# Moving seven of the modulation's twelve column sums between the stages, with three accumulators and two weight buffers

## The chip, the cores and the metric

One core of one Trainium2 chip runs the whole program. The metric is the device time of one execution, in microseconds (us). The engines are TensorE (PE, with its weight loads PEld), VectorE (DVE), ScalarE (ACT), GpSimd (POOL) and SyncE (SP), whose queue issues nearly all DMAs.

## What is computed

Two blocks follow one another on a sequence of 256 tokens of width 1024, all in float32. The first block is a mixer (eight attention heads and four mLSTM heads) and a squared-ReLU MLP of width 4096, each with a norm ahead and one behind. The second block has two layers with a modulation:

```python
c_act = jax.nn.silu(c)
for l in range(DEPTH_2):
    mod = c_act @ ada_w[l] + ada_b[l]
    shift1, scale1, gate1, shift2, scale2, gate2 = [
        m[:, None, :] for m in jnp.split(mod, N_MOD, axis=-1)]
    h = rms_norm_2(x, norm1_g[l]) * (1.0 + scale1) + shift1
    z = h @ w_in[l]
    ...
    x = x + (1.0 + gate1) * mixed
    h2 = rms_norm_2(x, norm2_g[l]) * (1.0 + scale2) + shift2
    f_gate, f_up = jnp.split(h2 @ w_ffn_in[l], 2, axis=-1)
    x = x + (1.0 + gate2) * ((jax.nn.silu(f_gate) * f_up) @ w_ffn_out[l])
return rms_norm_2(x, final_g)
```

`c` is one row of 1024 numbers and `ada_w[l]` is 1024 x 6144, so `mod` is a vector of 6144 numbers for each layer. It depends on nothing but inputs, and its weights are 2 x 24 MB.

## The kernel before, in words

**Weights in chunks.** All large products go over one list of 168 chunks (`plan`). A chunk is 512 columns of a weight by up to four tiles of 128 rows, 1 MB, and lands in one of three slots of `raw` (`RING = 3`). Each chunk is split for a product in three parts: ACT rounds it to `hi` (L830), DVE subtracts to get `lo` (L1203), and PE runs 48 matmuls (L425): `hi` by the activations' high part, `lo` by the high part, `hi` by the low part. PE's program is the list of chunks in order, so it is the order of everything else. Chunks 0 to 11 are the first mixer's inputs, 12 to 15 its output ("out", half), 16 to 31 ("up", g), 32 to 47 ("down", half); then layer 0: 48 to 65 its inputs, 66 to 69 two branches, 70 to 73 its output, 74 to 95 its FFN, 96 to 107 its down product (the last chunk of each half has two tiles); layer 1 is 108 to 167 in the same way.

**Who waits for what.** ACT and DVE run two chunks ahead (`LEAD = 2`): DVE's `advance(c)` makes `lo` of chunk c+2. ACT's `split(c)` needs the raw chunk landed and its slot of `hi` free, that is, chunk c-3 finished by PE. SP issues the load of chunk c once DVE has finished `lo` of chunk c-3.

**The modulation.** Its weights come in 96 pieces of 128 rows by 1024 columns (`ADA_W`), 512 KB each; eight pieces make one of twelve groups, and group 6 l + q is one sixth of layer l's `mod`. DVE multiplies a piece by `c_act` (one scalar for each partition) and adds it into an accumulator: L1222 for a group's first piece, L1224 for the others. There are two accumulators, taken in turn, and three buffers for pieces (`ADA_RING = 3`). After the eighth piece PE sums the accumulator over its partitions, 128 columns at a time: eight matmuls with one column of ones (L489), into PSUM bank 2. DVE adds the bias (`ada_columns`, L1212).

**Where they stand.** `ada_pos[j]` is the chunk at whose `advance` DVE works on piece j; `ada_at[c]` is the group that PE sums right after chunk c. Five groups are spread over chunks 14 to 45 (one piece a chunk up to 31, then three for two chunks), six over layer 0's FFN and down (three for two chunks), and one over layer 1's FFN. On SP's queue the piece stands three chunks ahead of its use, and the load of a chunk stands behind it:

```python
while j < pieces and ada_pos[j] + 3 == c:
    if j >= ADA_RING:
        sp.wait_ge(sem("ada_used"), j - ADA_RING + 1)
    sp.dma_start(ada_raw[:, j % ADA_RING, :], src)
    j += 1
...
sp.dma_start(raw[:, c % RING, 0:nk, at:at + w], src)
```

**Between stages.** At each norm PE sums squares (`sum_squares`, `sum_squares_late`, L503, L519 and L527), then ACT forms the root, DVE scales and ACT makes the high part, and only then can PE start the next product. In that time PE runs `keep_warm`: four matmuls of 256 columns whose result nobody reads (L534), eight ahead of ("up", 0).

## Time and profile before

| | us |
|---|---|
| median of three runs | 1131.62 |
| lowest and highest of them | 1130.69, 1134.76 |
| the profiled execution | 1129.57 |
| its span in the trace | 1127.7 |
| busy in the span: PE, DVE, ACT | 1095.7, 814.1, 520.3 |
| moved by DMA | 229.67 MB, mean 204 GB/s |

The 1.9 us between the profiled execution's time and its span are start and end of the program. A busy engine is not one that sets the time: what counts is whose work the others wait for at each place, which the chain of waits tells. PE's granted clock was 1.00 of full speed in all stretches shown below.

### The profile page before, as it was taken

The page shows a single profiled execution, that of the slowest core. Times are in us where ns is not written, and L with a number is a line of the kernel's source. Part 1 is how long each engine was busy: PE and PEld are TensorE (multiplying, and loading weights), DVE is VectorE, ACT ScalarE, POOL GpSimd, SP SyncE. Part 2 cuts the span into 40 slices and gives each one's busy share as a digit, 9 for nine tenths or more (in the row PEclk, how much of TensorE's full clock was granted, in tenths as well). Part 3 has the DMA queues.
Part 4 walks back from the last instruction along what each step waited for, and adds up shares of the span by engine and source line. Part 5 has one row for each costly group of instructions (what it writes and reads, how often), then busy time and mean ns, then how long its engine had stood idle before and what let it go on. Part 6 is the DMA issues. An engine that isn't in the chain of part 4 may idle for free.

```text
span 1127.7 us, 19577 instructions
## 1 busy us (share of the span) xinstructions
PE 1095.7 (97%) x8420; PEld 1038.0 (92%) x8420; DVE 814.1 (72%) x1078; ACT 520.3 (46%) x609; POOL 12.0 (1%) x26
## 2 busy tenths in 40 slices
PE   6999999999999999999999999999999999999998
PEld 5877889999998988989999999999898899999998
DVE  4865579887765898966778787859989477656452
ACT  4545566453433544554544443354345355444441
POOL 4000000000000000000000000000000000000000
PEclk9999999999999999999999999999999999999999
DMA  7545346887984453406698989946442376676551
GB/s 217 164 136 180 120 168 235 289 279 267 329 306 144 150 169 131 150 32 234 204 315 281 360 304 336 309 129 222 152 150 76 112 242 219 204 250 206 169 169 38
DMA packets 132078, 229.67 MB, mean 204 GB/s; under 512 B 5993, under 2 KB 59607, under 8 KB 131993
## 3 DMA queue, kind: packets, MB, share of 16 engines
q1 hardware_dynamic: 130404, 227.11, 59.7%
q8 instruction: 66, 1.08, 0.4%
q10 hardware_dynamic: 917, 1.27, 0.4%
q0 software_dynamic: 672, 0.06, 0.1%
q14 instruction: 19, 0.16, 0.0%
HBM read 227.35 MB, written 1.06 MB: 203 GB/s over the span
## 4 chain that ended last, share of the span: by engine, by line
PE 72%; DVE 19%; ACT 5%; issue 2%; DMA 2%; SPq 0%; DVEq 0%; ACTq 0%
PE mm L425 63%; DVE lo L1203 6%; DVE cacc L1283 5%; ACT hi L830 3%; PE pv L489 2%; PE mm L464 2%; DMA raw<-in_w_out_dram 1%; DVE ada_acc L1224 1%; DVE sB L1291 1%; PE pa L527 1%; PE pv L745 1%; PE pa L519 1%; DVE pB L1652 1%; DMA xin<-in_x_dram 1%; DVE qk L1307 0%
## 5 line engine op out<-in xcount | busy, mean ns | idle before, releaser
L425 PE MATMUL mm<-act_hi,hi 128*128 128x256 f32 x1760 | 490.9, 283 | 6.3 <-ACT act_hi L898 2.7
L425 PE MATMUL mm<-act_hi,lo 128*128 128x256 f32 x1760 | 484.7, 279 | 0.0
L1203 DVE TENSOR_TENSOR lo<-raw,hi 128x2048 fp32r<-128x2048 f32 (+1 forms) x160 | 361.8, 2265 | 161.9 <-ACT hi L830 159.9
L425 PE MATMUL mm<-act_lo,hi 128*128 128x256 f32 x1760 | 467.4, 279 | 0.0
L830 ACT ACTIVATE hi<-raw 128x2048 fp32r<-128x2048 f32 (+1 forms) x160 | 301.5, 1890 | 240.2 <-PE mm L425 188.5
L425 PEld LDWEIGHTS mm<-act_hi,hi 128*128 128x128 f32 x1760 | 330.9, 188 | 12.5 <-issue 8.8
L425 PEld LDWEIGHTS mm<-act_hi,lo 128*128 128x128 f32 x1760 | 330.9, 188 | 0.9 <-issue 0.7
L425 PEld LDWEIGHTS mm<-act_lo,hi 128*128 128x128 f32 x1760 | 320.5, 188 | 0.0
L425 PE MATMUL mm<-u_hi,hi 128*128 128x256 f32 x608 | 170.7, 281 | 0.0
L425 PE MATMUL mm<-u_hi,lo 128*128 128x256 f32 x608 | 169.7, 279 | 0.0
L425 PE MATMUL mm<-u_lo,hi 128*128 128x256 f32 x608 | 169.7, 279 | 0.0
L425 PEld LDWEIGHTS mm<-u_hi,lo 128*128 128x128 f32 x608 | 114.3, 188 | 0.1
L425 PEld LDWEIGHTS mm<-u_hi,hi 128*128 128x128 f32 x608 | 114.3, 188 | 0.1
L425 PEld LDWEIGHTS mm<-u_lo,hi 128*128 128x128 f32 x608 | 114.3, 188 | 0.0
L1224 DVE SCALAR_TENSOR_TENSOR ada_acc<-ada_raw,ca,ada_acc 128x1024 f32<-128x1024 f32 x84 | 107.6, 1281 | 1.3 <-DMA ada_raw<-in_ada_w_dram 0.3
L1283 DVE SCALAR_TENSOR_TENSOR cacc<-cu,convw,cacc 128x256 f32<-128x256 f32 x240 | 98.9, 479 | 2.4
L1151 ACT ACTIVATE sq<-mm 128x512 f32<-128x512 f32 x22 | 13.2, 599 | 60.5 <-PE mm L425 60.5
L909 ACT ACTIVATE pB<-sB,small 128x128 f32<-128x128 f32 (+1 forms) x32 | 14.3, 449 | 50.4 <-DVEq L1295 50.4
L1251 DVE TENSOR_TENSOR u_lo<-sq,u_hi 128x512 fp32r<-128x512 f32 (+1 forms) x30 | 25.0, 835 | 16.9 <-ACT u_hi L902 16.6
L902 ACT ACTIVATE u_hi<-sq 128x512 fp32r<-128x512 f32 x22 | 13.9, 633 | 43.9 <-DVEq L1713 43.9
L1601 DVE SCALAR_TENSOR_TENSOR x<-mm,cols,x 128x256 f32<-128x256 f32 x32 | 14.0, 480 | 27.5 <-PE mm L425 26.9
L425 PE MATMUL mm<-on,raw 128*128 128x256 f32 x128 | 29.1, 380 | 0.2
(254 smaller groups left out, 962.3 us busy)
## 6 DMA issues: line engine op xcount, KB each, us to landing
ada_raw<-in_ada_w_dram SPq DMA_DIRECT2D x96, 512.0 KB, 6.2
raw<-in_w_ffn_in_dram SPq DMA_DIRECT2D x88, 512.0 KB, 5.8
raw<-in_w_in_dram SPq DMA_DIRECT2D x40, 1024.0 KB, 5.1
raw<-in_w_ffn_out_dram SPq DMA_DIRECT2D x20, 1024.0 KB, 5.9
raw<-in_w_up_dram SPq DMA_DIRECT2D x16, 1024.0 KB, 6.7
raw<-in_w_down_dram SPq DMA_DIRECT2D x16, 1024.0 KB, 7.8
raw<-in_w_out_dram SPq DMA_DIRECT2D x12, 1024.0 KB, 5.1
raw<-in_w_in_dram SPq DMA_DIRECT2D x16, 512.0 KB, 6.1
```

The lines of the kernel that those rows point to most:

```text
L425: ins = pe.matmul(o, w[:, kk, fs], a[:, k, :], start=(k == 0 and i == 0 and f % 2 == 0), stop=(ends and i == len(pairs) - 1), skip_group_c ...
L464: ins = pe.matmul(mm[:, b0 + tt, :], a[:, k, tok], w[:, kk, :], start=(k == 0 and i == 0), stop=(ends and i == 2), skip_group_check=True)
L489: ins = pe.matmul(b[:, f:f + 1], ada_acc[:, i % 2, f * P:(f + 1) * P], ones[:, 0:1], start=(f == 0), stop=True, skip_group_check=True)
L830: a(act.activation(hi[:, c % RING, 0:nk, :], raw[:, c % RING, 0:nk, :], ACT.Copy), "hi_done")
L902: a(act.activation(dst, src, ACT.Copy, scale=scale), done)
L909: a(act.activation(p[:, i, lo_:hi_], s[:, i, lo_:hi_], ACT.Exp, scale=-1.0, bias=small[:, 2 + 2 * i + q:3 + 2 * i + q], accum_out=small[:, ...
L1151: a(act.activation(sq[:, 0:2, :], complete((l, "ffn", g))[:, 0, :], other(ACT.Silu)), "silu_gate_ready")
L1203: v(dve.tensor_tensor(lo[:, c % RING, 0:nk, :], raw[:, c % RING, 0:nk, :], hi[:, c % RING, 0:nk, :].bitcast(F32), ALU.subtract), "lo_done")
L1224: link(dve.scalar_tensor_tensor(out=acc, in0=w, scalar=ca[:, 1, k:k + 1], in1=acc, op0=ALU.mult, op1=ALU.add), "ada_used")
L1251: ins = dve.tensor_tensor(d_lo, src, h, ALU.subtract)
L1283: v(dve.scalar_tensor_tensor(out=cacc[:, k, :], in0=src, scalar=w, in1=cacc[:, k, :], op0=ALU.mult, op1=ALU.add), name)
L1601: ins = dve.scalar_tensor_tensor(out=x[:, k, :], in0=tile_of(src, f), scalar=gain[:, k:k + 1], in1=x[:, k, :], op0=ALU.mult, op1=ALU.add)
```

## The change

Seven groups (0, 3, 4, 5, 9, 10 and 11) are no longer summed after a chunk but between stages: group 0 ahead of ("up", 0), groups 3 and 4 ahead of layer 0's input, 5 ahead of layer 0's FFN, 9 and 10 ahead of layer 1's input, 11 ahead of layer 1's FFN. The groups 1, 2, 6, 7 and 8 stay after chunks 22, 30, 79, 85 and 90. `keep_warm` is shorter at four of these places and gone at one. The eight pieces of group 0 stand at chunks 4 to 11, inside the first mixer, and all others move up by eight, so layer 1's FFN has none. There is a third accumulator (4 KB a partition), and `ada_raw` has two buffers in place of three.

```diff
--- before.py
+++ after.py
@@ -53,7 +53,8 @@
 ADA_W = D
 ADA_T = ADA_W // P
 ADA_GROUPS = MODS // ADA_T
-ADA_RING = 3
+ADA_RING = 2
+ADA_ACCS = 3
 ADA_P = KD
 LAMBDA_INIT = [0.8 - 0.6 * float(np.exp(-0.3 * l)) for l in range(LAYERS)]
 MAGIC = 1.5 * 2.0 ** 23
@@ -177,17 +178,20 @@
 
     first = {name: ids[0] for name, (_, ids) in groups.items()}
     pieces = LAYERS * ADA_GROUPS * ADA_P
-    stages = [(range(groups[("out", 0)][1][1], first[(0, "in", 3)]), 5, lambda c: 0.85 if c < first[("down", 0)] else 1.3)]
-    for l, after_ffn in ((0, 6), (1, 1)):
-        stages.append((range(first[(l, "ffn", 0)], first[(1, "in", 3)] if l == 0 else first[(1, "down", 0)]), after_ffn,
-                       lambda c: 1.0 if c < first[(0, "down", 0)] else 0.9))
+    stages = [(range(first[("in", 2)], first[("out", 1)] + 1), 1, lambda c: 1.0),
+              (range(groups[("out", 0)][1][1], first[(0, "in", 3)]), 5, lambda c: 0.85 if c < first[("down", 0)] else 1.3),
+              (range(first[(0, "ffn", 0)], first[(1, "in", 3)]), 6, lambda c: 1.0 if c < first[(0, "down", 0)] else 0.9)]
+    ada_between = {first[("up", 0)]: (0, 0, 1), first[(0, "in", 3)]: (0, 3, 2), first[(0, "ffn", 0)]: (0, 5, 1),
+                   first[(1, "in", 3)]: (1, 3, 2), first[(1, "ffn", 0)]: (1, 5, 1)}
+    later = {(l, q + i) for l, q, count in ada_between.values() for i in range(count)}
     ada_pos, ada_at = [], {}
     for window, count, share in stages:
         until = np.cumsum([share(c) for c in window[:-2]])
         for j in range(count * ADA_P):
             ada_pos.append(window[int(np.searchsorted(until, (j + 0.5) / (count * ADA_P) * until[-1]))])
-            if j % ADA_P == ADA_P - 1:
-                ada_at[ada_pos[-1] + 1] = divmod(len(ada_pos) // ADA_P - 1, ADA_GROUPS)
+            l, q = divmod(len(ada_pos) // ADA_P - 1, ADA_GROUPS)
+            if j % ADA_P == ADA_P - 1 and (l, q) not in later:
+                ada_at[ada_pos[-1] + 1] = l, q, 1
 
 
 
@@ -242,7 +246,7 @@
         hi = sb("hi", [P, RING, CK, GF], F32R)
         lo = sb("lo", [P, RING, CK, GF], F32R)
         ada_raw = sb("ada_raw", [P, ADA_RING, ADA_W])
-        ada_acc = sb("ada_acc", [P, 2, ADA_W])
+        ada_acc = sb("ada_acc", [P, ADA_ACCS, ADA_W])
         cst = sb("cst", [P, C_ALL])
         x = sb("x", [P, KD, S])
         act_hi = sb("act_hi", [P, KD, S], F32R)
@@ -480,15 +484,21 @@
                             ins.then_inc(sem(done), 1)
                 ins.then_inc(sem("mm_done"), 1)
                 if c in ada_at:
-                    l, q = ada_at[c]
-                    i = l * ADA_GROUPS + q
-
+                    ada_sums(c, ada_at)
+
+            def ada_sums(c, where, part=None):
+
+                l, q, count = where[c]
+                for a in range(count) if part is None else (part,):
+                    i = l * ADA_GROUPS + q + a
                     pe.wait_ge(sem("ada_used"), (i + 1) * ADA_P)
-                    b = bank(2)
+                    b = bank(2) if a == 0 else pv[2]
                     for f in range(ADA_T):
-                        ins = pe.matmul(b[:, f:f + 1], ada_acc[:, i % 2, f * P:(f + 1) * P], ones[:, 0:1], start=(f == 0), stop=True,
+                        to = a * ADA_T + f
+                        ins = pe.matmul(b[:, to:to + 1], ada_acc[:, i % ADA_ACCS, f * P:(f + 1) * P], ones[:, 0:1], start=(to == 0), stop=True,
                                         skip_group_check=True)
-                    full(ins, 2)
+                    if a == count - 1:
+                        full(ins, 2)
 
             def product(name, *acts, **kw):
                 for j in range(len(groups[name][1])):
@@ -691,7 +701,8 @@
             out_pieces(0, (4, 5, 6, 7))
             chunk(("out", 1), 1, act_hi, act_lo)
             sum_squares_late(((6, 7),))
-            keep_warm(WARM + 4)
+            ada_sums(first[("up", 0)], ada_between)
+            keep_warm(WARM + 0)
             for g in range(8):
                 product(("up", g), act_hi, act_lo, ready="norm_ready" if g == 0 else None)
                 if g == 0:
@@ -706,9 +717,12 @@
             for late in (True, False):
                 if late:
                     sum_squares_late(((6, 7),))
+                    ada_sums(first[(0, "in", 3)], ada_between, 0)
+                    keep_warm()
                 else:
                     sum_squares()
-                keep_warm()
+                    ada_sums(first[(0, "in", 3)], ada_between, 1)
+                    keep_warm(2)
 
 
             for l in range(LAYERS):
@@ -777,14 +791,15 @@
                     for half in range(2):
                         chunk((l, "out", half), j, act_hi, act_lo, ready=None if half else "mixed_split", per=2)
                 sum_squares_late()
-                keep_warm()
+                ada_sums(first[(l, "ffn", 0)], ada_between)
+                keep_warm(2)
                 for g in range(11):
                     product((l, "ffn", g), act_hi, act_lo, ready="norm_ready" if g == 0 else None)
                 product((l, "down", 0), u_hi, u_lo, ready="u_ready", per=2)
                 if l < LAYERS - 1:
                     product((l, "down", 1), u_hi, u_lo)
                     sum_squares_late()
-                    keep_warm()
+                    ada_sums(first[(1, "in", 3)], ada_between)
 
             def turn_output(kh, to):
 
@@ -1205,16 +1220,16 @@
 
             def ada_columns(c):
 
-                if c not in ada_at:
-                    return
-                l, q = ada_at[c]
-                mc = slice(l * MODS + q * ADA_T, l * MODS + (q + 1) * ADA_T)
-                link(dve.tensor_tensor(modT[:, mc], full(2)[:, 0:ADA_T], adabT[:, mc], ALU.add), "bank2_free")
+                for where in (ada_at, ada_between):
+                    if c in where:
+                        l, q, count = where[c]
+                        mc = slice(l * MODS + q * ADA_T, l * MODS + (q + count) * ADA_T)
+                        link(dve.tensor_tensor(modT[:, mc], full(2)[:, 0:count * ADA_T], adabT[:, mc], ALU.add), "bank2_free")
 
             def ada_piece(j):
 
                 i = j // ADA_P
-                acc = ada_acc[:, i % 2, :]
+                acc = ada_acc[:, i % ADA_ACCS, :]
                 dve.wait_ge(sem(f"ada_loaded{j % ADA_RING}"), 16 * (j // ADA_RING + 1))
                 k = j % ADA_P
                 w = ada_raw[:, j % ADA_RING, :]
```

Two places show what moved. The first is PE's program at the norm ahead of layer 1's input product, behind the last chunk of layer 0's down product. Before:

```order
L425 MATMUL mm<-u_hi,hi 128x256
L425 MATMUL mm<-u_hi,lo 128x256
L425 MATMUL mm<-u_lo,hi 128x256
L527 MATMUL pa<-sq,cst 128x256 x4
L534 MATMUL pv<-cst 128x256 x4
L425 MATMUL mm<-act_hi,hi 128x256
L425 MATMUL mm<-act_hi,lo 128x256
```

With the change (L537 and L498 are the lines that were L527 and L489):

```order
L429 MATMUL mm<-u_hi,hi 128x256
L429 MATMUL mm<-u_hi,lo 128x256
L429 MATMUL mm<-u_lo,hi 128x256
L537 MATMUL pa<-sq,cst 128x256 x4
L498 MATMUL pv<-cst,ada_acc 128x1 x16
L429 MATMUL mm<-act_hi,hi 128x256
L429 MATMUL mm<-act_hi,lo 128x256
```

The sixteen matmuls of groups 9 and 10 stand in the place of the four of `keep_warm`; their former places, each eight matmuls after a chunk of layer 0's down product, hold nothing now.

The second is DVE's program in the first mixer, at the step of chunk 4 (`advance(4)`). `nlam<-pv` frees PSUM bank 2 for PE's next product. Before:

```order
L1307 TENSOR_TENSOR qk<-qk,hf 128x512
L1203 TENSOR_TENSOR lo<-raw,hi 128x2048
L1376 COPY nlam<-pv 128x2
L1291 ISA sA,small<-pv,cst 128x128
L1291 ISA small 128x1
L1291 ISA sA,small<-pv,cst 128x256
```

With the change:

```order
L1322 TENSOR_TENSOR qk<-qk,hf 128x512
L1218 TENSOR_TENSOR lo<-raw,hi 128x2048
L1237 TENSOR_SCALAR ada_acc<-ada_raw,ca 128x1024
L1391 COPY nlam<-pv 128x2
L1306 ISA sA,small<-pv,cst 128x128
L1306 ISA small 128x1
L1306 ISA sA,small<-pv,cst 128x256
```

The first piece of group 0 (L1237, which was L1222) now stands ahead of that copy; seven more follow, one at each of the next seven chunks. SP's program has the same kinds of entries in the stages that follow; what differs there is the number that each piece waits for.

## Rows read from the trace of the kernel before

**Rows 1.** the chain of waits that ended last, by engine

```profile
PE 72%; DVE 19%; ACT 5%; issue 2%; DMA 2%; SPq 0%; DVEq 0%; ACTq 0%
```

**Rows 2.** by stretch: PE, PEld, DVE, ACT, POOL busy, clock, DMA share, GB/s

```profile
255.00:350.00 95.00, 95.00 (x819) 95.00 (x818) 67.56 (x46) 35.13 (x24) 0.00 (x0) 1.00 0.85 295
600.00:660.00 60.00, 60.00 (x518) 60.00 (x517) 48.60 (x39) 24.64 (x21) 0.00 (x0) 1.00 0.95 318
940.00:1040.00 100.00, 100.00 (x860) 100.00 (x859) 63.20 (x46) 45.80 (x37) 0.00 (x0) 1.00 0.70 227
```

**Rows 3.** the chain of waits in order of time: start, us, what

```profile
161.25 3.45 PE pv L534 x16
...
581.87 1.29 DVE ada_acc L1224
583.21 1.95 PE pv L489 x16
585.15 33.72 PE mm L425 x288
618.87 1.68 PE pv L489 x16
```

**Rows 4.** timeline, PE at the norms ahead of two products

```profile
546.07 1.89 PE L534 MATMUL pv<-cst 128*128 128x256 f32 x8
...
548.48 0.35 PE L425 MATMUL mm<-act_hi,hi 128*128 128x256 f32 x1 [0.52 <-ACT act_hi L898]
...
748.29 1.89 PE L534 MATMUL pv<-cst 128*128 128x256 f32 x8
...
751.11 0.36 PE L425 MATMUL mm<-act_hi,hi 128*128 128x256 f32 x1 [0.93 <-ACT act_hi L898]
```

**Rows 5.** timeline, first mixer: DVE's nlam and PE's gate product

```profile
59.78 0.15 DVE L1376 COPY nlam<-pv 128x2 f32<-128x2 f32 x1
...
60.08 3.62 PE L621 MATMUL pv<-hng,wg 128*36 128x256 f32 x16 [1.29 <-DVE nlam L1376]
```

**Rows 6.** waits of the SP queue: waited for, us in total, times, longest

```profile
SPq L373 <- DVE ada_acc L1224: 184.3, 74, 6.5
```

**Rows 7.** timeline, layer 0's FFN: the two pieces that bound a loop

```profile
615.27 1.28 DVE L1224 SCALAR_TENSOR_TENSOR ada_acc<-ada_raw,ca,ada_acc 128x1024 f32<-128x1024 f32 x1
...
628.44 1.28 DVE L1224 SCALAR_TENSOR_TENSOR ada_acc<-ada_raw,ca,ada_acc 128x1024 f32<-128x1024 f32 x1
```

**Rows 8.** timeline, layer 0's down: one loop (DVE, SP, ACT, DVE)

```profile
667.26 2.60 DVE L1224 SCALAR_TENSOR_TENSOR ada_acc<-ada_raw,ca,ada_acc 128x1024 f32<-128x1024 f32 x2
...
668.93 0.43 SPq L383 DMA_DIRECT2D raw<-in_w_ffn_out_dram  x1
...
675.57 1.92 ACT L830 ACTIVATE hi<-raw 128x2048 fp32r<-128x2048 f32 x1 [2.46 <-DMA raw<-in_w_ffn_out_dram]
...
679.80 1.28 DVE L1224 SCALAR_TENSOR_TENSOR ada_acc<-ada_raw,ca,ada_acc 128x1024 f32<-128x1024 f32 x1
```

**Rows 9.** timeline, first block's down: one loop (DVE, SP, DVE)

```profile
285.60 0.75 DVE L1222 TENSOR_SCALAR ada_acc<-ada_raw,ca 128x1024 f32<-128x1024 f32 x1
...
286.74 0.44 SPq L383 DMA_DIRECT2D raw<-in_w_down_dram  x1
...
299.45 1.28 DVE L1224 SCALAR_TENSOR_TENSOR ada_acc<-ada_raw,ca,ada_acc 128x1024 f32<-128x1024 f32 x1
```

**Rows 10.** landing of raw in 440 to 470, of ada_raw at 250.9

```profile
DMA to landing us min/median/max: 4.9/5.0/5.0
...
DMA to landing us min/median/max: 3.7/3.7/3.7
```

**Rows 11.** timeline, DVE's low parts in layer 0's FFN: first, third and fifth

```profile
578.34 2.29 DVE L1203 TENSOR_TENSOR lo<-raw,hi 128x2048 fp32r<-128x2048 f32 x1 [1.18 <-ACT hi L830]
...
589.49 2.29 DVE L1203 TENSOR_TENSOR lo<-raw,hi 128x2048 fp32r<-128x2048 f32 x1 [1.18 <-ACT hi L830]
...
601.38 2.29 DVE L1203 TENSOR_TENSOR lo<-raw,hi 128x2048 fp32r<-128x2048 f32 x1 [1.18 <-ACT hi L830]
```


## Prediction

> **What bounds the kernel now.** I read the chain of waits by engine first: TensorE (PE) holds 72% of it and VectorE (DVE) 19% [rows 1]. The table of stretches then says where PE stands without a gap: in the first block's down products, in the FFN of layer 0 and in that of layer 1 PE is busy for the whole stretch at a granted clock of 1.00, while the DMA share is 0.85, 0.95 and 0.70 [rows 2]. So in these stages only work taken off PE, or a wait put in front of it, moves the time; and in two of them the DMA engines are nearly full. The chain in order of time gives PE's rhythm: 288 matmuls in 33.72 us, which is six chunks of 48, so 5.62 us a chunk and **11.24 us for two**, and between them a column sum of 1.68 us that nothing hides [rows 3].
>
> **The change part by part.**
>
> *Seven column sums leave the chunk stream.* Each of the twelve sums is eight matmuls of L489 (16 records), 1.68 us on the chain [rows 3]. Three leave the first block's down products, three layer 0's FFN and down, one layer 1's FFN: 7 x 1.68 = **-11.8 us**.
>
> *They come back at five places between stages.* There PE waits for the norm and runs filler (L534: eight of them, 16 records, take 3.45 us, so 0.43 each [rows 3]). From the first filler matmul to the first matmul of the FFN it is 2.41 us in layer 0, and 2.82 us ahead of layer 1's input product [rows 4]. Ahead of both FFNs and at the second place ahead of layer 0's input, PE now has 1.68 + 2 x 0.43 = 2.54 us to do: 0.13 us too much, three times (I take the places not shown as like the one shown). Ahead of ("up", 0), eight fillers become one sum and four fillers, 3.40 for 3.45 us: nothing. The other place ahead of layer 0's input has one sum and its old four fillers, in a wait for x: nothing. Ahead of layer 1's input there are two sums, 3.36 us in 2.82: 0.54. Together **+0.9 us**. If a norm were ever shorter than its filler, each sum would cost its 1.68.
>
> *Eight pieces move into the first mixer.* A piece is one DVE instruction of 1.28 us (0.75 for the first of eight). Layer 1's FFN loses eight; PE did not wait for them there. The first new one stands on DVE between the low part of a chunk and the copy of nlam, which ends when PE starts L621 [rows 5]: **+0.8 us**. The other seven come once a chunk, where PE has a whole chunk of matmuls in front of it and DVE idles; I cost them at nothing (bounds: 0 and 7 x 1.28 = 9.0 us). Their DMAs go ahead of the weight chunks on SP's queue, whose chunks there are long landed when ACT takes them.
>
> *Two weight buffers for three.* This is the edit that decides. SP issues piece j ahead of the chunk three places on, and the next chunk's load is queued behind it. With three buffers, j waits until DVE has used piece j-3, with two until j-2. Even now SP waits 184 us in all for pieces [rows 6]. In the stretches with three pieces to two chunks, piece j-3 nearly always belongs to the chunk five ahead of the one loaded, whose low part the load waits for anyway; j-2 belongs to the chunk four ahead. That closes a loop over **two** chunks: piece used, ada and raw transfer, ACT's high part, DVE's low part, next piece used. It must fit into 11.24 us.
>
> The trace of before holds three such loops, at places where two chunks with two pieces each follow one another:
> - FFN: piece ended at 615.27 + 1.28 = 616.55, next piece ended at 628.44 + 1.28 = 629.72: **13.17 us** [rows 7].
> - down of layer 0: first of two pieces ended at 668.54, raw issued at 668.93, next piece ended at 681.08: **12.54 us** [rows 8].
> - down of the first block: 286.35 to 300.73, **14.38 us** [rows 9]; older loads were still under way, so it is the upper bound.
>
> The lower bound is from idle stretches: a piece alone lands 3.7 us after its issue, a raw chunk alone in 5.0 [rows 10], so another half megabyte costs 1.3 and both together 6.3 us. In the loop of layer 0's down, ACT starts at 675.57, released by the landing, and the loop closes 5.51 us later [rows 8]; with 6.3 and 0.04 for handing over that is **11.85 us**. All four are longer than 11.24. I take 13.17 in the FFN and 12.54 in the down products, since these were measured in the same stages.
>
> Layer 0, chunks 81 to 107: 7.5 loops x 1.93 + 6 loops x 1.30 = 22.3 us late. PE has slack first: the low part of chunk 80 ends at 580.63 [rows 11] and PE starts on that chunk at 585.15 [rows 3], 4.5 us; and two sums that still stand in the stream (3.4 us) give the loads time. 22.3 - 4.5 - 3.4 = 14.4. The sum after chunk 79 already waits for its last piece (that piece ends at 581.87 + 1.29 = 583.16, the sum starts at 583.21 [rows 3]), so the first late loads go straight into PE: three loads each 1 to 3 us late, I take 2. Layer 0: **+16.4 us**. First block, chunks 35 to 47: 6.5 x 1.30 = 8.5 us, less a slack of 6.6 that is PE's lead in steady state (11.24 less 1.92 for the high part, 2.29 for the low part [rows 8, 11] and 0.4 that I allow for handing over): **+1.9 us**. In ("up", g) there is one piece a chunk, j-2 lies five ahead, and a loop over three chunks has 16.9 us: nothing.
>
> Sum: -11.8 + 0.9 + 0.8 + 16.4 + 1.9 = **+8.2 us** on the profiled execution's 1129.6. The median of the runs shown is 1131.6, 2.0 above it; on that the forecast is **1140 us**.
>
> *A rule of the Trainium skill.* All three measured loops overrun the two chunks [rows 7 to 9]. "Trainium Kernel Development and Optimization", Best Practices, advises to double-buffer for performance, that is, that two buffers overlap DMA and compute; by it the stalls of 16.4 and 1.9 would not be, and the sum would be -10.1, about the time of the first rival below. The trace speaks against it here, since the third buffer is what now keeps the loop at three chunks.
>
> **Rivals.**
>
> *The transfers land sooner (faster).* With fewer loads under way at once, each may land as in an idle stretch. The place is the same loop, the price 11.85 - 11.24 = 0.6 us each: 13.5 x 0.6 = 8.2, less the slack of 7.9, is 0.3; 1 us at the sum after chunk 79, 1 for unevenness; nothing in the first block. Sum -11.8 + 1.7 + 2.3 = -7.8, **1124 us**. It decides below a loop of about 12.0 us. For it: the ring itself thins the queue. Against it: the bytes stay, and the DMA share is 0.95 at 318 GB/s [rows 2]; the loops of 13.17 and 12.54 had little else queued [rows 7, 8]. "DMA: Bandwidth & Descriptors", Anatomy of one DMA, fits a transfer by 2.0 us and its bytes over 436 GB/s; that is an estimate of 5.6 us for both transfers, a loop of 11.2, and a sum of -10.1.
>
> *The sums are not hidden between stages.* The change would then not do what it says: seven sums at full price give -11.8 + 11.8, and with a loop that costs nothing the time is **1132 us**, no change. Against it: fillers stand there, and no work waits for them [rows 4].
>
> *The queue never empties.* If every loop takes 14.38 us, layer 0 costs 13.5 x 3.14 - 7.9 + 2 = 36.5 and the first block 6.5 x 3.14 - 6.6 = 13.8: -10.1 + 50.3, **1172 us**. Against it: 14.38 was measured with an older load still landing.
>
> A fourth thing is no rival but a floor: where three pieces fall on two chunks, DVE and ACT alone need 11.15 and 11.89 us from one low part to the next but one [rows 11], so even with free transfers the sums taken out are not all gained.
>
> **How the numbers follow.** The forecast's case has 0.77: loops of 12.2 to 13.4 us give 1129 to 1152, of which 0.14 lies within 0.5% (5.7 us; about what a measurement of this kernel can tell from no change) and 0.63 above. Transfers that land sooner: 0.13, nearly all below 1126. Sums not hidden: 0.05, no change. Queue never empties: 0.05. So faster 0.12, same 0.20, slower 0.68. The range from 1126 to 1152 leaves out the fast rival for the most part, and the slowest.
>
> **What would show it.** Right: in layer 0's FFN and down products PE waits for the low part of the chunks from about 88 on, some 1 us for every two or three; ACT's high parts wait for DMA before nearly every chunk; SP's wait for pieces grows from 184 us to well over 250; the DMA share falls there; between stages L489's sums fill the place of fillers and the first matmul comes at most 0.6 us later; the first mixer is 1 us longer; layer 1's FFN is 1.7 us shorter. Wrong: PE is without gaps in layer 0 and raw transfers land in under 5.5 us there (the fast rival), or the five places are each over 1.5 us longer, or a gap opens in the first mixer.

## The result, and the profile after

| | before | after |
|---|---|---|
| median of the runs, us | 1131.15 (1130.12 to 1134.76) | 1168.37 (1158.30 to 1172.63) |
| ratio, 95% interval | | 1.0312 (1.0276 to 1.0347) |
| profiled execution, its span, us | 1129.57, 1127.7 | 1167.03, 1165.2 |

The change is 3.1% slower: 37 us, against a sum of 8.2 us in the forecast and a range that ended 16 us lower. The sign was right, the size was not.

Chain of waits by engine, after (to be read beside [rows 1]):

```profile
PE 47%; DVE 23%; DMA 15%; ACT 9%; issue 4%; SPq 1%; ACTq 0%; DVEq 0%
```

PE no longer holds the chain: DMA has gone from 2% to 15%, ACT from 5% to 9%. The next table cuts each trace at the first product matmul of five stages, first before, then after. Columns: from and to; length; PE busy (and its instructions); PEld, DVE, ACT, POOL busy; granted clock; DMA share; GB/s. The stages are ("up", 0) to layer 0's input, its input to its FFN, FFN to layer 1's input, that to its FFN, and the rest.

```profile
164.40:367.80 203.40, 200.08 (x1666) 196.97 (x1665) 154.85 (x126) 91.77 (x79) 0.00 (x0) 1.00 0.75 260
367.80:548.50 180.70, 177.72 (x1249) 163.39 (x1249) 143.54 (x262) 89.00 (x126) 0.00 (x0) 1.00 0.46 155
548.50:751.10 202.60, 200.63 (x1700) 199.19 (x1701) 158.79 (x139) 85.49 (x74) 0.00 (x0) 1.00 0.85 289
751.10:931.20 180.10, 177.62 (x1249) 163.30 (x1249) 143.56 (x262) 89.01 (x126) 0.00 (x0) 1.00 0.47 155
931.20:1127.70 196.50, 191.52 (x1640) 191.12 (x1640) 108.81 (x97) 81.84 (x72) 0.00 (x0) 0.99 0.55 180
```

```profile
169.70:376.40 206.70, 198.91 (x1646) 195.31 (x1645) 154.77 (x125) 91.63 (x79) 0.00 (x0) 1.00 0.77 259
376.40:556.20 179.80, 178.01 (x1262) 164.31 (x1261) 143.61 (x263) 89.04 (x126) 0.00 (x0) 1.00 0.45 153
556.20:785.50 229.30, 210.50 (x1678) 208.13 (x1677) 162.62 (x147) 87.57 (x79) 0.00 (x0) 0.95 0.79 262
785.50:968.70 183.20, 180.92 (x1262) 167.09 (x1262) 139.70 (x253) 86.53 (x120) 0.00 (x0) 0.98 0.43 144
968.70:1165.20 196.50, 191.57 (x1626) 191.08 (x1624) 99.70 (x89) 81.79 (x72) 0.00 (x0) 0.99 0.50 161
```

So +5.3 us have come up to ("up", 0), +3.3 in the first block's MLP, -0.9, **+26.7** in layer 0's FFN and down, +3.1 at the start of layer 1, and 0 in the rest, where one sum of 1.68 should have gone. It has gone, but the same matmuls were slower in this execution: from the first product of layer 1's FFN to the small matmuls of L810 it is 178.4 us without any wait and at clock 1.00, against 176.8 in two later runs with the same schedule (194.9 us for the whole stage) and 178.4 before, with the sum in it. Two traces of kernels that keep the sum there, four sums and ring of two alone, show the same step, 180.1 for 178.4. Why PE is 0.9% slower in some executions at full clock stays open.

In layer 0's FFN and down the time that PE is not busy grows from 2.0 to 18.8 us, and PE's busy time from 200.6 to 210.5 us although it runs fewer instructions: the mean granted clock was 0.95 in place of 1.00.

The predicted loop is there. This is the chain of waits after, in layer 0's FFN (start, us, what):

```profile
635.14 1.21 DVE ada_acc L1239
636.37 0.34 SPq L377
...
636.75 0.43 SPq L387
...
637.23 6.31 DMA raw<-in_w_ffn_in_dram
...
643.55 1.93 ACT hi L845
...
645.58 2.29 DVE lo L1218
647.87 1.21 DVE ada_acc L1239
649.09 0.34 SPq L377
...
649.48 0.43 SPq L387
...
649.95 7.27 DMA raw<-in_w_ffn_in_dram
...
657.24 1.93 ACT hi L845
...
663.16 0.43 SPq L387
```

The piece is used, SP issues a piece (L377) and behind it the weight chunk (L387), that lands, ACT (L845) and DVE (L1218) split it, and the next piece is used. From one issue of a chunk to that of the next but one: 649.48 - 636.75 = 12.73 us, then 13.68. PE wants 11.24 for two chunks [rows 3]. From chunk 78 on ACT starts nearly every high part within 0.1 us of the chunk's landing. The waits of SP's queue for the use of a piece (us in total, times, longest):

```profile
SPq L377 <- DVE ada_acc L1239: 324.5, 70, 16.7
```

It was 184.3 us before [rows 6], and "well over 250" was what the prediction asked for.

What was not predicted is in the first mixer. Timeline after, DVE, ACT and PE (in brackets: idle before, and what ended it):

```profile
93.25 2.29 DVE L1218 TENSOR_TENSOR lo<-raw,hi 128x2048 fp32r<-128x2048 f32 x1 [3.68 <-ACT hi L845]
95.46 1.28 DVE L1239 SCALAR_TENSOR_TENSOR ada_acc<-ada_raw,ca,ada_acc 128x1024 f32<-128x1024 f32 x1
...
96.77 0.29 DVE L1306 CUSTOM_DVE_ANT_0 sA<-pv,cst 128x128 f32<-128x128 f32 x1
...
97.51 0.40 ACT L924 ACTIVATE pA<-sA,small 128x128 f32<-128x128 f32 x1 [4.29 <-DVEq L1310]
...
97.56 0.34 PE L688 MATMUL pv<-cst,gate 4*128 4x4 f32 x2 [4.97 <-DVE small L1306]
```

DVE works on the moved piece before it forms the softmax maximum (L1306). ACT has waited 4.29 us for that maximum with its exponentials (L924), and ACT's next high part stands behind them, so DVE's next low part comes later by the piece, and the next maximum too: a circle of ACT and DVE that the piece makes longer at each turn, not once. The low parts show it: counted from the first product, seven of them in a row (from the one at 48.0 us before) come 1.1, 2.2, 3.6, 5.0, 6.2, 8.1 and 8.9 us later than before. PE stands 4.97 us at L688, and its clock is 0.50 for 6.8 us, from 95 us on. The two small matmuls were without a gap before:

```profile
94.36 0.28 PE L678 MATMUL pv<-cst,gate 4*128 4x4 f32 x2
94.58 0.50 PE L464 MATMUL mm<-hi,act_hi 128*128 128x512 f32 x1
```

From the first product to ("up", 0) it is 164.4 - 21.5 = 142.9 us before and 169.7 - 18.7 = 151.0 after: 8.1 us more. (The first product itself began 2.8 us earlier in this execution; that is not part of the change's work.)

And ahead of layer 1's input, after:

```profile
776.61 2.42 PE L537 MATMUL pa<-sq,cst 128*128 128x256 f32 x8 [3.60 <-ACT sq L906]
778.82 6.82 PE L498 MATMUL pv<-cst,ada_acc 128*128 128x1 f32 x32
785.50 0.56 PE L429 MATMUL mm<-act_hi,hi 128*128 128x256 f32 x1
785.86 0.41 PE L429 MATMUL mm<-act_hi,lo 128*128 128x256 f32 x1
```

The two sums, 32 records, take 6.8 us where I had reckoned 3.4, and the product behind them goes at 0.41 us a matmul for 0.28: the granted clock was at the lower of its levels, 1.2 of 2.4 GHz, from 778.0 for 13.7 us. Of these, 6.2 us lie in the next stage and cost it 3.1, which is all that it is longer. PE had also stood 3.60 us ahead of L537 here, for ACT's square of the late last chunk, so this trace alone does not say what the sums have to do with it.

### The profile page after: what moved, and what is told of

It reads as the page before. It is cut to its first block, busy times and chain, and to the rows that moved or that the text cites. A ratio compares the mean times of both kernels' runs of the same rounds, so it can differ in the third digit from the quotient of the medians.

```text
span 1165.2 us, 19517 instructions
## 1 busy us (share of the span) xinstructions
PE 1109.3 (95%) x8392; PEld 1051.6 (90%) x8392; DVE 814.3 (70%) x1076; ACT 519.8 (45%) x609; POOL 12.2 (1%) x26
## 4 chain that ended last, share of the span: by engine, by line
PE 47%; DVE 23%; DMA 15%; ACT 9%; issue 4%; SPq 1%; ACTq 0%; DVEq 0%
PE mm L429 41%; DVE lo L1218 8%; ACT hi L845 6%; DMA raw<-in_w_ffn_in_dram 5%; DVE cacc L1298 4%; DMA raw<-in_w_down_dram 4%; DVE ada_acc L1239 3%; DMA raw<-in_w_ffn_out_dram 3%; DMA raw<-in_w_in_dram 1%; PE pv L498 1%; DMA ada_raw<-in_ada_w_dram 1%; PE pa L537 1%; DVE sB L1306 1%; PE mm L468 1%; SPq L377 1%
## 5 line engine op out<-in xcount | busy, mean ns | idle before, releaser
L1218 DVE TENSOR_TENSOR lo<-raw,hi 128x2048 fp32r<-128x2048 f32 (+1 forms) x160 | 361.9, 2265 | 201.4 <-ACT hi L845 199.8
L429 PE MATMUL mm<-act_hi,hi 128*128 128x256 f32 x1760 | 496.6, 286 | 5.1 <-DVE lo L1218 4.2
L845 ACT ACTIVATE hi<-raw 128x2048 fp32r<-128x2048 f32 (+1 forms) x160 | 301.9, 1890 | 284.3 <-PE mm L429 106.3
L429 PEld LDWEIGHTS mm<-act_hi,hi 128*128 128x128 f32 x1760 | 335.2, 190 | 9.9 <-issue 6.3
L429 PEld LDWEIGHTS mm<-act_hi,lo 128*128 128x128 f32 x1760 | 335.4, 191 | 1.0 <-issue 0.7
L429 PEld LDWEIGHTS mm<-act_lo,hi 128*128 128x128 f32 x1760 | 323.9, 190 | 0.0
L924 ACT ACTIVATE pB<-sB,small 128x128 f32<-128x128 f32 (+1 forms) x32 | 14.3, 449 | 50.4 <-DVEq L1310 50.4
L498 PEld LDWEIGHTS pv<-cst,ada_acc 128*128 128x128 f32 x192 | 27.1, 222 | 4.2 <-DVE ada_acc L1239 3.7
L1727 DVE TENSOR_TENSOR sq<-sq,mm 128x512 f32<-128x512 f32 x22 | 15.1, 687 | 21.8 <-ACT sq L1166 21.4
```

What stands on the lines that cost most here:

```text
L429: ins = pe.matmul(o, w[:, kk, fs], a[:, k, :], start=(k == 0 and i == 0 and f % 2 == 0), stop=(ends and i == len(pairs) - 1), skip_group_c ...
L498: ins = pe.matmul(b[:, to:to + 1], ada_acc[:, i % ADA_ACCS, f * P:(f + 1) * P], ones[:, 0:1], start=(to == 0), stop=True, skip_group_check ...
L845: a(act.activation(hi[:, c % RING, 0:nk, :], raw[:, c % RING, 0:nk, :], ACT.Copy), "hi_done")
L924: a(act.activation(p[:, i, lo_:hi_], s[:, i, lo_:hi_], ACT.Exp, scale=-1.0, bias=small[:, 2 + 2 * i + q:3 + 2 * i + q], accum_out=small[:, ...
L1218: v(dve.tensor_tensor(lo[:, c % RING, 0:nk, :], raw[:, c % RING, 0:nk, :], hi[:, c % RING, 0:nk, :].bitcast(F32), ALU.subtract), "lo_done")
L1727: link(dve.tensor_tensor(sq[:, 4:6, :], sq[:, 0:2, :], src[:, 1, :].rearrange("p (a s) -> p a s", a=2), ALU.mult), *freed((l, "ffn", g)))
```

## The experiments

Times are medians; each ratio is to the kernel before on the same chip, and the median of before lay between 1130.9 and 1131.6 us throughout.

### One part of the change at a time

**Ring of two alone.**

```diff
-ADA_RING = 3
+ADA_RING = 2
```

> The kernel before with two weight buffers for three and nothing else. Theory A (the loop over two chunks, closed on SP's queue, makes the loss): the first block's down products 6 to 9 us longer, layer 0's FFN and down 26 to 32 us longer, 1163 to 1172 us in all. Rival B (the loss comes from the eight pieces in the first mixer and from sums at half clock between stages): 1131 to 1145 us.

Measured: **1157.6 us**, 1.0234 (1.0191 to 1.0277), from two executions only; some 26 us more, a little under what theory A asked for and far from B. The two stages with three pieces to two chunks, in its trace:

```profile
161.70:369.80 208.10, 202.25 (x1667) 198.73 (x1665) 154.85 (x126) 91.78 (x79) 0.00 (x0) 0.99 0.76 257
...
550.60:776.30 225.70, 210.53 (x1701) 207.57 (x1701) 159.11 (x140) 85.05 (x74) 0.00 (x0) 0.96 0.80 263
```

Layer 0's FFN and down take 23.1 us more than before. PE runs as many instructions, 1701 for 1700, but they take 210.5 us for 200.6: 13.2 us of the loss is idling and 9.9 longer work, most of it clock (17 us of this stage are at 0.50, which costs 8.5). The trace has five stretches at 0.50 between 300 and 1100 us, at 317.5, 587.1, 696.4, 733.9 and 771.5, and each begins within 3 us of the end of a wait of PE of 1.4 to 3.0 us. So a gap costs PE its own length and, behind it, matmuls at half clock. My sum had only the first. The stretch at 771.5 stands ahead of layer 1's input, with the old filler there: a gap of 1.82 us was enough.

**Four sums between the stages and nothing else**: three buffers, two accumulators, no piece moved. Groups 3 and 4 are summed ahead of layer 0's input, 9 and 10 ahead of layer 1's.

> Three buffers and two accumulators as before, no piece moved; only groups 3 and 4 are summed ahead of layer 0's input and groups 9 and 10 ahead of layer 1's, in the place of all or part of the filler. Theory A: 4 x 1.68 us less in the chunk stream, at most 0.6 us more at each place, 1125 to 1126 us. Rival B (sums between stages cost as much as in the stream, or run at half clock): 1130 us or more.

Measured: 1127.4 us, 0.9969 (0.9954 to 0.9983): 4 us gained where 6 were due. In the first block and at layer 0's input the sums do what the prediction said (199.8 us for 203.4, two sums less), but at layer 1's input:

```profile
737.14 1.13 PE L536 MATMUL pa<-sq,cst 128*128 128x256 f32 x4 [0.16 <-ACT sq L903]
738.10 4.43 PE L497 MATMUL pv<-cst,ada_acc 128*128 128x1 f32 x32
742.39 0.56 PE L428 MATMUL mm<-act_hi,hi 128*128 128x256 f32 x1
```

The stretches around it (columns as above):

```profile
736.00:740.70 4.70, 4.54 (x33) 3.94 (x33) 4.48 (x8) 2.33 (x6) 0.00 (x0) 1.00 0.06 7
740.70:744.00 3.30, 3.30 (x17) 3.30 (x17) 3.19 (x9) 2.19 (x5) 0.00 (x0) 0.50 0.89 310
744.00:747.50 3.50, 3.50 (x19) 3.50 (x18) 2.43 (x6) 2.67 (x4) 0.00 (x0) 0.50 0.01 4
747.50:752.00 4.50, 4.50 (x40) 4.50 (x40) 2.29 (x1) 2.87 (x2) 0.00 (x0) 0.99 0.00 0
```

PE has no gap of note there (0.16 us), and yet its clock is 0.50 from 740.7 to 747.5, over the sums' end and the first product matmuls.

**One sum fewer at that place, with filler behind it.**

```diff
-first[(1, "in", 3)]: (1, 3, 2)
+first[(1, "in", 3)]: (1, 4, 1)
...
 ada_sums(first[(1, "in", 3)], ada_between)
+keep_warm(2)
```

> Three buffers, two accumulators, no piece moved: two sums at layer 0's input as in the four-sums run, but only one at layer 1's input, and two fillers of 256 columns behind it; the other is back in the stream. Theory A, the half clock after the two sums ahead of layer 1's input came from one-column matmuls standing where filler stood: no stretch at half clock near 740 us; 3 x 1.68 = 5.0 leave the stream, first product matmul at most 0.3 us later: 1126.5, not slower than the four sums (1127.4). Rival, the clock falls there whatever PE runs: half clock again near 740, 1129 or more.

Measured: **1126.2 us**, 0.9965 (0.9950 to 0.9981). The stretch around the place:

```profile
741.00:752.00 11.00, 10.84 (x82) 10.01 (x81) 10.11 (x21) 6.39 (x13) 0.00 (x0) 1.00 0.30 98
```

The half clock is gone there. The total, with one sum more in the stream, is about that of the four sums; the intervals do not part the two.

**One-column filler in the kernel before**, which measures the disputed cost by itself:

```diff
-keep_warm()
+pe.wait_ge(sem("bank1_free"), n.seen("bank1"))
+for _ in range(16):
+    pe.matmul(pv[1][:, 0:1], ident, cst[:, C_ID:C_ID + 1], start=True, stop=True)
```

> The kernel before, with the eight filler matmuls of 256 columns ahead of layer 1's input replaced by sixteen of one column, which take as long as two sums (3.4 us) and wait for nothing. Theory A, one-column matmuls there let the clock fall: half clock from about 749 us for 3.4 us or more, layer 1's first product matmuls at half clock, 0.5 us for the length and 2 to 4 us for the clock: 1134 to 1136. Rival, the half clock of the four-sums run came from the sums' own wait or place: clock 1.00 there, 1131.5 to 1132.5.

Measured: 1134.3 us, 1.0023 (1.0010 to 1.0036), 3.4 us more, as theory A has it.

```profile
748.26 3.98 PE L789 MATMUL pv<-cst 128*128 128x1 f32 x32
752.11 0.56 PE L425 MATMUL mm<-act_hi,hi 128*128 128x256 f32 x1
752.47 0.41 PE L425 MATMUL mm<-act_hi,lo 128*128 128x256 f32 x1
```

(The wait for bank 1 is that of `keep_warm`.) Nothing waits for these matmuls, and the trace has no idle time ahead of them; the product starts 1.0 us later and then runs at 0.41 us a matmul.

### What the first mixer costs

**The maximum ahead of the piece**, in the changed kernel:

```diff
-advance(groups[name][1][j])
+advance(groups[name][1][j], pieces_too=False)
...
+if i < len(todoA):
+    ada_pieces(groups[name][1][j])
```

(the second part stands behind the maximum).

> The changed kernel, but in the first mixer DVE does a unit's softmax maximum ahead of the unit's piece. Theory: there ACT and DVE work in one circle (maximum, exponentials, high part, low part, piece), the piece lengthens it by 1.28 us and PE ends up waiting 5 us for bank 0, with 3.4 us more of half clock behind it; with the maximum first, the gap ahead of the output product of unit 3 (now 7.8 us between matmuls of the product, 2.7 before) goes back to under 3.5, and the time falls by 5 to 7 us. Rival: the gap is a late DMA or the gates' rows; it stays, and so does the time.

Measured: 1161.5 us, 1.0269 (1.0241 to 1.0297): 7 us less than the change. From the first product to ("up", 0) it is 163.2 - 19.3 = 143.9 us: 1.0 more than in the profiled execution before, 0.8 more than the 143.1 in the traces of four and of three sums, which have no moved piece. The seven low parts come 0.9 to 1.0 us later than before and no longer fall further behind. That fits the 0.8 I had put down for the piece ahead of nlam; the 7 us were the circle.

**Three buffers and the changed schedule**, two accumulators, groups 4 and 5 summed together, one sum with two fillers at layer 1's input; first with the maximum ahead, then with the piece ahead.

> Three buffers, two accumulators, and the changed kernel's schedule: eight pieces in the first mixer with the softmax maximum ahead of each, one sum ahead of (up, 0), two at layer 0's input, one with two fillers at layer 1's input, none in layer 1's FFN. Theory A (loss of the change = ring of two + the circle of ACT and DVE in the mixer + half clock at layer 1's input, and nothing else in it): four sums leave the stream, -6.7, the first piece +0.8, places +0.2: 1126. Rival C, the schedule itself costs more (the remaining pieces in the mixer, or the loads they bring, hold PE): over 1131, with PE waits between 60 and 165 us of the trace.

> As the run that had the maximum first and three buffers (1126.3), but each piece in the first mixer ahead of the softmax maximum again, as the change has it. Theory A, the circle of ACT and DVE (maximum, exponentials, turned copy, high part, low part, piece, next maximum) is what costs in the mixer, whatever the ring: a gap of over 5 us in PE's product matmuls between 90 and 100 us, half clock behind it, and 6 to 8 us more: 1132 to 1134. Rival, the gap needed late loads from the ring of two: no gap, within 1.5 us of 1126.3.

Measured: **1126.3 us**, 0.9954 (0.9937 to 0.9970), and 1133.4 us, 1.0015 (0.9998 to 1.0032). The order alone is worth 7 us with three buffers too, so the gap needs no late load:

```profile
98.78 0.34 PE L687 MATMUL pv<-cst,gate 4*128 4x4 f32 x2 [4.54 <-DVE small L1305]
```

### Why two buffers cost so much

**The pieces on POOL's queue.** SP issues weight chunks only; POOL waits until DVE has made the low part of the chunk ahead of the piece's own and until a buffer is free, and issues the piece.

> The changed kernel with the pieces issued from the POOL queue, each once DVE has made the low part of the chunk ahead of its own and used piece j-2; SP issues only chunks. Theory A1 (it is the queue: the chunk's load stands behind the piece's wait): loads leave three chunks ahead again, PE's gaps in layer 0 go, 1126 to 1136 us, the first mixer's gap of 5 us stays. Theory A2 (it is the buffer count: pieces land late whichever queue issues them, and DVE's low parts stand behind them): 1150 us or more.

Measured: 1163.8 us, 1.0289 (1.0260 to 1.0318), hardly better than the change. The waits have moved:

```profile
DVE ada_acc L1238 <- DMA ada_raw<-in_ada_w_dram: 63.7, 29, 5.2
```

ACT's waits for the weights of layer 0's FFN, its down product and the first block's down product fall from 36.7, 41.1 and 57.4 us to 5.9, 8.3 and 4.6, and DVE now waits 63.7 us for pieces. From this I drew that two buffers are too few whatever the order. That was wrong.

**The chunk ahead of the piece, on SP's queue.** The loads of `raw`, with the wait for the chunk's own slot, are moved ahead of the `while` that issues pieces (the semaphore increments are left out here):

```diff
+for at, w, src in parts:
+    sp.dma_start(raw[:, c % RING, 0:nk, at:at + w], src)
 while j < pieces and ada_pos[j] + 3 == c:
     ...
-for at, w, src in parts:
-    sp.dma_start(raw[:, c % RING, 0:nk, at:at + w], src)
```

> The changed kernel with SP's order turned: a weight chunk is issued ahead of the pieces that stood in front of it, so a piece that waits for its buffer holds up only the chunk after. Theory A, with two buffers a piece can land only after its predecessor but one is used, whatever the order; the wait moves from ACT's high part to VectorE's piece, as on POOL's queue: within 8 us of the change, 1158 to 1170, and VectorE waits over 40 us for piece landings. Theory B, the order on SP's queue is the price: 1145 or less.

Measured: **1132.9 us**, 1.0021 (1.0002 to 1.0040), 35 us less than the change: theory B, and well below its 1145. The stage with the largest loss, and DVE's wait for pieces:

```profile
547.50:751.00 203.50, 200.75 (x1679) 199.45 (x1677) 160.41 (x139) 85.34 (x76) 0.00 (x0) 0.98 0.86 291
```

```profile
DVE ada_acc L1239 <- DMA ada_raw<-in_ada_w_dram: 24.3, 30, 2.4
```

DVE waits for 30 pieces here, about as often as on POOL's queue, but at most 2.4 us, and PE waits only 0.4 us for low parts and 2.1 for one sum in that stage. A piece that has to wait for its buffer now holds up the chunk after, which has time; before, it held up the chunk that was wanted next. SP's queue in this run:

```profile
649.77 1.71 SPq L379 DMA_DIRECT2D raw<-in_w_ffn_in_dram  x2
651.52 6.41 SPq L386 DMA_DIRECT2D ada_raw<-in_ada_w_dram  x2
657.97 1.16 SPq L379 DMA_DIRECT2D raw<-in_w_ffn_in_dram  x2
```

SP stands at the pieces (L386) until 657.97 as it did in the change, but ACT's waits for these weights are 2.1 us in all.

**The same in the kernel before with two buffers.**

> The kernel before with two piece buffers, and SP issuing each weight chunk ahead of the pieces that stood in front of it. With two buffers and the old order it took 26 us more. Theory B, the price of the ring is the order on SP's queue: at most 3 us above the kernel before, 1130 to 1134. Theory A, the ring of two costs by the late pieces themselves, and the change with the order turned gained by something else: 1145 or more.

Measured: 1137.6 us, 1.0054 (1.0038 to 1.0070). Neither theory had this: it is 3 us above the range of B and far below A. The order is some 20 of the 26 us; 6.7 stay with the ring of two itself. In the trace PE waits 4.0 us in layer 0's FFN and down for two sums whose last piece is late, and 10.2 us there are at half clock.

**A quarter of each piece transferred**, before with three buffers, before with two, the change, and the pieces on POOL's queue. These kernels leave out three quarters of each piece's transfer, so their modulation is not the reference's; DVE does the same work:

```diff
-sp.dma_start(ada_raw[:, j % ADA_RING, :], src)
+w = ADA_W if j < ADA_RING else ADA_W // 4
+sp.dma_start(ada_raw[:, j % ADA_RING, 0:w], src[:, 0:w])
```

> The kernel before, but from the fourth piece on only a quarter of each modulation piece is transferred (128 KB in place of 512 KB; the rest of the buffer keeps what it had, so the modulation is not the reference's); VectorE does the same work. It is the base for the next run. Both theories: within 4 us of the kernel before (1131.5), since PE does not wait for loads there: 1128 to 1132.

> The same with two piece buffers in place of three (a quarter of each piece transferred, modulation not the reference's). With full pieces the ring of two alone cost 26 us. Theory A, the loop of two chunks is too long by its transfers: a piece of a quarter of the bytes shortens the loop by about 1 us (1.3 us for half a megabyte, three quarters of it), so at least half of the cost goes: 0 to 12 us above the run with three buffers, 1130 to 1142. Theory B, it is the order of issue and the hand-overs (SP stands behind the use of a piece, whatever the bytes): 20 us or more above the run with three buffers, over 1150.

> The changed kernel, but from the third piece on only a quarter of each modulation piece is transferred (the modulation is not the reference's). Theory A, the parts add up: the ring of two costs 26 us with full pieces and 3 with quarters, so 23 of it go, while the mixer's circle (7) and layer 1's half clock (4) stay: 1168.4 - 23 = 1145, range 1139 to 1149. Rival, the sums between the stages and the third accumulator cost by themselves over 10 us: over 1152.

> The pieces on POOL's queue, two buffers, and from the third piece on a quarter of each piece transferred (modulation not the reference's). Theory C, a queue of its own did not help because a piece goes from the use of its last but one to its own use in 0.56 + 0.53 + 5.0 us there against 0.03 + 0.34 + 5.3 on SP, and with the 1.28 of its own that leaves nothing of the 7.49 that two pieces have: with transfers 2.5 us shorter VectorE no longer waits for pieces, and the time falls by 25 us or more from 1163.8, to 1131 to 1138. Rival, POOL's part costs otherwise (its writes to the queue stand in VectorE's way): over 1150.

| | whole pieces | quarters |
|---|---|---|
| before | 1131 | 1130.8, 0.9994 (0.9984 to 1.0005) |
| before, two buffers | 1157.6 | 1133.8, 1.0025 (1.0013 to 1.0037) |
| the change | 1168.4 | 1135.3, 1.0038 (1.0018 to 1.0059) |
| the change, POOL's queue | 1163.8 | 1142.3, 1.0081 (1.0054 to 1.0108) |

With three buffers the bytes cost nothing. With two, three quarters of the bytes are worth 24 us, and in the change 33, 10 more than expected. So the transfer inside the loop is the price, and with a transfer that I estimate to be 1 us shorter (1.3 us for half a megabyte, three quarters of it) the loop hardly holds PE. On POOL's queue it falls by 21.5 us, short of the 25 I asked for but far from the rival's 1150. A possible reason why that queue failed with whole pieces: from the release of a buffer to POOL's issue it takes 0.56 us, from there to the landing 5.6 in the median of layer 0's FFN and down (0.53 of it the issue), and 1.28 for the use: 7.4 us, with 7.5 to be had when three pieces go with two chunks in 11.24. On SP with the order turned these are 0.03, 5.6 (0.34 of it the issue) and 1.28: 6.9. That this half microsecond is all of it, I have not shown.

### The repairs together

**The change with both orders turned**, and then with one sum and two fillers at layer 1's input as well.

> The changed kernel with both repairs: weight chunk ahead of the pieces on SP's queue, softmax maximum ahead of the piece in the first mixer. If the two are independent: 1132.9 - 7 = 1126, range 1124 to 1128. Rival, the repairs overlap (the gap in the mixer took loads' lateness with it): 1130 or more.

> The same with one sum and two fillers of 256 columns in place of two sums ahead of layer 1's input (the other sum back in the stream). Theory A, one-column sums let the clock fall there: no half clock at the start of layer 1, 1.7 more in the stream and 2 to 5 less at the place: 0 to 3 us below the run before, 1123 to 1126. Rival, no clock effect: 1.1 to 1.7 us above it.

Measured: 1127.5 us, 0.9966 (0.9947 to 0.9986), and 1129.3 us, 0.9973 (0.9956 to 0.9990). The two orders add up: 1132.9 less 5.4. The last step brings nothing, as its rival had it. Layer 1's input stage is indeed 2.8 us shorter (180.7 for 183.5), but the sum that went back into the stream waits 1.76 us for its last piece, at 682 us, and 6.8 us of half clock follow. No version beats 1126, which three buffers give with three or four sums moved, 5 us below the kernel before.

## Why the prediction missed

Two steps failed. The term for the ring of two, +18.3 us in the sum, priced a gap of PE by its length alone; the ring costs 26 us by itself and the order on SP's queue 35 in the change. And the seven pieces in the first mixer, taken at nothing, cost 7 us.

**Ring of two (+16.4 and +1.9): right in place and mechanism, half in size.** The loops in layer 0's FFN were as taken: on the chain, from the load issued at 572.21 to that at 678.34 us, there are eight, of 12.3 to 15.2 us, 13.3 in the mean, against 13.17. In its down product the three that the chain shows whole are 13.5 to 14.6 us, against 12.54; others there were shorter. PE begins to wait for the low part at 656 us, chunk 90, as forecast ("from about 88 on"), though with 0.16 us there; waits of 1 us and more come from 684 us on, the longest, 5.6 us, at 738. Its idle time is about as summed: 16.8 us more in that stage (3.6 of it at the place ahead of layer 1's input), against 16.4. What the step left out is the clock. PE's busy time rose by 9.9 us there, though three sums (5.0 us) had left the stream for two at the stage's end in place of filler (3.4 for 1.9 us at full clock), and by 9.9 in the ring-only run with nothing moved. In the profiled execution of before the clock had been 1.00 in that stage [rows 2], where PE stood 2.0 us in all, and I took that for a property of the stage. In the first block the idle time grew by 4.5 us for the 1.9 forecast: the six loops on the chain there were 12.0 to 14.3 us, 13.2 in the mean, longer than the 12.54 that I carried over from layer 0; the 14.38 of [rows 9], which I had set aside, was not far off. In all, quarters give back 33 us and the turned order 35, for 18.3 in the sum. (The 3.7 us for "a piece alone" [rows 10], on which the lower bound rests, was not read in an idle stretch: a chunk was issued right behind that piece, at 251.29.)

**The sums that leave the stream (-11.8): not gained while the loop sets the pace.** With three buffers four moved sums gave 4 of 6 us. In the change six of the seven leave stages in which PE waits for loads; there a sum fills time in which the next chunk is on its way, and PE waits that much longer without it. I had allowed for this with the two sums that stayed, not with the six that went. It would be why the ring alone costs 26 us in the kernel before and 33 to 35 in the change; that is an argument, no run shows it by itself. What fits it: with both orders turned the loads no longer set the pace, and the change is 3.4 us below the kernel before, where the sum without the ring is -10.1 and two buffers with the turned order cost 6.7. The floor of 11.15 and 11.89 us that the prediction gave DVE and ACT was none: these were distances at PE's own pace, and with the turned order PE waits 0.4 us for low parts in that stage.

**First mixer (+0.8, and +0 for seven pieces): failed.** A gap there stood among the prediction's own signs of being wrong. "Where PE has a whole chunk of matmuls in front of it and DVE idles": both true, and both beside the point, since DVE idled because it waited for ACT, which waited for DVE. The upper bound I gave, 9.0 us, was nearer than the value taken; 7 us were measured with two and with three buffers, and 5.4 between the runs with the order on SP's queue turned.

**The five places (+0.9): right at layer 0, wrong at layer 1's input.** The stage that ends ahead of layer 0's FFN has no loss (179.8 for 180.7 us). Ahead of layer 1's input I compared durations, 3.36 against 2.82 us, and took one filler for as good as another. Two sums in a row with no filler stood there in eight traces, and all eight have half clock at the place, for 3.4 to 17.1 us; so has one-column filler, at a cost of 3.4 us. The four traces with one sum and 256-column filler have none. In the change a gap of 3.60 us comes on top, and no run parts the two.

**Transfers and buffers.** The loads on the chain took 6.31, 7.27, 6.75 and 8.27 us from the end of their issue. The fit of the Trainium skill, "DMA: Bandwidth & Descriptors", Anatomy of one DMA, is for one DMA issued by GpSimd; taken for both transfers on SP's queue it gave an estimate of 5.6 us, and this trace does not bear that out while both are under way. The Trainium skill, "Trainium Kernel Development and Optimization", Best Practices, advises to double-buffer so that DMA and compute overlap; by the 1157.6 us that is not enough with the old order on SP's queue, and by the 1137.6 us nearly enough with the other.

**The rival of 1172 us** came nearest in number, by luck: it wanted every loop at 14.38 us, where 13.3 and 13.2 were the means in layer 0's FFN and the first block, and had neither clock nor mixer. What its number should have told is that three terms (the first block's loops, the mixer, layer 1's place) had been taken at or near their low end, and that no gap had been given a price beyond its length.

**The ledger**, from single runs: 1131.2; +26.5 ring of two; +7 mixer; +3.4 one-column sums at layer 1's input; makes 1168.1, against 1168.4. Part of this fit is luck. It holds only if the sums taken out gained nothing in the end, which the point above argues and no single run shows; and the half clock at layer 1's input came from a gap too, of which the ring's 26.5 may already have a share.

## What to carry to other kernels

When a buffer count is cut, look first at what stands behind the waiting instruction on its queue: the same two buffers cost 26 us with the wanted load behind the wait and 7 with it ahead. A gap in PE costs more than its length where it is followed by matmuls at half clock, so a stage that shows 1.00 now is no base for what it will be once PE stands; here 13.2 us of idling came with 9.9 us of longer work. And before idle time of an engine is filled, find out whom it waits for: if the two wait for each other in turn, each microsecond put between them comes back at every turn.

## What was not expected of the hardware

- The granted clock fell to 0.50 with no gap of note in PE's work: from 740.7 us in the run of four sums and from 751.4 for 6.8 us with one-column filler. In both it fell while PE was running 32 records of one-column matmuls.
- Short stretches at 0.50, mostly 3.4 or 6.8 us, stood in all traces (in the profiled execution of before only one, at the very end); the mean granted clock over the span is 0.995 with two buffers and quarter pieces, 0.988 with two buffers and whole ones, 0.980 in the change and 0.998 in the profiled execution of before, whose other executions have 0.993 to 0.998 but for one. The same wait does not always bring one: ahead of the sum after chunk 79 PE stands 0.88 us both before and with three sums, and only the second has half clock behind it, for 3.4 us.
- Times of one kernel spread by up to 12.5 us (leaving out two single executions of 2779 and 2194 us), which makes differences under 2 us unsafe here.
- A DMA issue took 0.53 us on POOL's queue against 0.34 on SP's, and came 0.56 us after its release against 0.03.
